# Feature sums of the two later norms in strips of 32 columns, in a two-layer hybrid decoder step on one Trainium2 core

## What is computed

```python
def layer_norm(x, g=None, b=None):
    xf = x.astype(jnp.float32)
    mu = jnp.mean(xf, axis=-1, keepdims=True)
    var = jnp.mean(jnp.square(xf - mu), axis=-1, keepdims=True)
    y = (xf - mu) * lax.rsqrt(var + LN_EPS)
    ...

def trunk_layer(x, c, pos, lw, st, mla_past):
    mod = jax.nn.silu(c) @ lw['w_ada'] + lw['b_ada']
    sh1, sc1, g1, sh2, sc2, g2 = jnp.split(mod[:, None, :], 6, axis=-1)
    u = x * (1.0 + sc1) + sh1
    mix, new_st = mixer_branches(u, pos, lw, st, mla_past)
    x = layer_norm(DEEPNORM_ALPHA * x + g1 * mix, lw['ln1_g'], lw['ln1_b'])
    u2 = x * (1.0 + sc2) + sh2
    f = (jax.nn.silu(u2 @ lw['w1']) * (u2 @ lw['w3'])) @ lw['w2']
    x = layer_norm(DEEPNORM_ALPHA * x + g2 * f, lw['ln2_g'], lw['ln2_b'])
    return x, new_st
```

## Time and profile before

| what | value |
|---|---|
| median of 3 runs | 1809.6 us (1809.22 to 1810.36) |
| the profiled execution | 1809.78 us, its span 1808.0 us |
| PE busy | 1703.8 us, 94% of the span |
| DVE, ACT, POOL busy | 809.4, 733.8, 705.7 us |
| granted clock of PE, mean | 0.971 of full speed |
| output projection, layer 0 | ends at about 635.8 us; norm 1 until about 655 us |
| second FFN product, layer 0 | ends at about 908.5 us |
| second FFN product, layer 1 | ends at about 1786.3 us; the span ends at 1808.0 us |

### The profile page before, as it was taken

The page is one execution under the profiler, slowest core; times in us unless marked ns, Lnnn a source line. Parts: engine busy times, 40 slices in busy tenths (PEclk is TensorE's granted clock), DMA queues, the critical chain, the costliest instruction groups (busy, mean ns, idle before and its releaser), DMA issues. The chain is left out here.

```text
span 1808.0 us, 29755 instructions
## 1 busy us (share of the span) xinstructions
PE 1703.8 (94%) x10994; PEld 1475.5 (82%) x10994; DVE 809.4 (45%) x1881; ACT 733.8 (41%) x1109; POOL 705.7 (39%) x446
## 2 busy tenths in 40 slices
PE   5999999999999979999979999999999999899997
PEld 2887889886667869998867879898866687799996
DVE  2364276656431353332255534866744323533223
ACT  2455534233434244442344554442344332444422
POOL 2344556636123423333323435655541234333331
PEclk8999999999999989999999999999999999899999
DMA  8365435337575344445624553362566834344440
GB/s 352 108 250 187 122 98 192 132 120 268 185 273 178 130 172 155 148 159 198 210 103 184 199 186 92 122 205 78 169 243 230 292 133 174 134 150 144 160 140 30
DMA packets 73522, 307.68 MB, mean 170 GB/s; under 512 B 15842, under 2 KB 25506, under 8 KB 43426
## 3 DMA queue, kind: packets, MB, share of 16 engines
q1 hardware_dynamic: 73378, 305.77, 48.3%
HBM read 291.81 MB, written 13.94 MB: 169 GB/s over the span
## 5 line engine op out<-in xcount | busy, mean ns | idle before, releaser
L2154 POOL TENSOR_TENSOR wlx<-ring,wh 128x1024 fp32r<-128x1024 f32 x172 | 409.6, 2381 | 659.2 <-ACT wh L1168 651.8
L454 PE MATMUL zps<-uhi,wh 128*128 128x320 f32 x1232 | 386.9, 326 | 0.2
L455 PE MATMUL zps<-ulo,wh 128*128 128x320 f32 x1232 | 372.4, 314 | 0.0
L1168 ACT ACTIVATE wh<-ring 128x1024 fp32r<-128x1024 f32 x172 | 182.2, 1060 | 363.5 <-PE zps L455 222.5
L2268 POOL TENSOR_TENSOR wlo<-ring,whi 128x1024 fp32r<-128x1024 f32 x66 | 160.1, 2426 | 318.2 <-ACT whi L1131 317.9
L454 PEld LDWEIGHTS zps<-uhi,wh 128*128 128x128 f32 x1232 | 238.5, 194 | 14.1 <-issue 7.7
L455 PEld LDWEIGHTS zps<-ulo,wh 128*128 128x128 f32 x1232 | 238.6, 194 | 1.2 <-issue 0.4
L938 PE MATMUL zps<-xhi,whi 128*128 128x320 f32 x688 | 214.0, 311 | 0.0
L939 PE MATMUL zps<-xlo,whi 128*128 128x320 f32 x688 | 213.8, 311 | 0.0
L940 PE MATMUL zps<-xhi,wlo 128*128 128x320 f32 x688 | 213.7, 311 | 0.0
L459 PE MATMUL zps<-uhi,wlx 128*128 128x320 f32 x1232 | 207.6, 311 | 0.0
(11 more groups left out here) (285 smaller groups left out, 2503.5 us busy)
## 6 DMA issues: line engine op xcount, KB each, us to landing
ring<-wpack_dram SPq DMA_DIRECT2D x222, 1024.0 KB, 4.9
arena<-cache_dram SPq DMA_DIRECT2D x128, 320.0 KB, 4.9
arena<-stateA_dram SPq DMA_DIRECT2D x2, 2064.0 KB, 9.5
o_cn_s<-arena SPq DMA_DIRECT2D x2, 2064.0 KB, 11.6
arena<-stateD_dram SPq DMA_DIRECT2D x2, 2048.0 KB, 11.7
o_ret_s<-arena SPq DMA_DIRECT2D x2, 2048.0 KB, 10.9
x<-x_dram SPq DMA_DIRECT2D x2, 1280.0 KB, 9.9
o_y<-x SPq DMA_DIRECT2D x4, 640.0 KB, 3.0
```

The lines of the kernel that those rows point to most:

```text
L454: nc.tensor.matmul(o, hi[:, k * P:(k + 1) * P], xh[:, k, :], start=k == 0, stop=False)
L455: last = nc.tensor.matmul(o, hi[:, k * P:(k + 1) * P], xl[:, k, :], start=False, stop=False)
L1168: nc.scalar.activation(wh[:, i, :], ring[:, g % RING, i * 1024:(i + 1) * 1024], ACT.Copy).then_inc(*ev("act_hq", (q, i), layer=layer))
L2154: G().tensor_tensor(low_ring(SPLIT[q])[:, half], ring_of(SPLIT[q])[:, half], wh[:, i, :], ALU.subtract).then_inc(*ev("pool_l", (q, i)))
```

## The change

The 128x128 matrix of ones is no longer the weight operand in the two norms. Instead:

- Each product uses 32 columns of ones, so its result has 32 rows, and goes into one of four strips of 32 partitions of the bank: tile k into strip k mod 4 (`strip_sum`). Each strip holds the sum of two tiles, the same in its 32 rows.
- ACT copies the bank of four strips to SBUF (`mean_strips` into std, and one more line in `squares` into tmp), and one more f32 product with a constant 128x128 matrix of 1/32 (`gather`) adds the four strips up and spreads the sum to all partitions. This holds for the mean and for the squares.
- In the second FFN product the products of the mean for k = 0 to 5 now stand behind the tiles d = 2 to 7, as they did in the output projection already; before, all came after the last tile. In both, k = 6 no longer waits for the last residual.
- `gather` takes the place of `ones` in the packed constants, but is loaded with the later part; the early part holds the identity alone. The ones are now taken from another constant that holds them anyway.

```diff
-    c["ones"] = np.ones((P, P), f)
+    c["gather"] = np.full((P, P), 1 / 32, f)
...
-        ident, ones = cs("ident"), cs("ones")
+        ident, gather = cs("ident"), cs("gather")
+        ones = cs("causal")[:, P:2 * P]
...
+                    def strip_sum(ps, src, k):
+
+                        g = 32 * (k % 4)
+                        return nc.tensor.matmul(ps[g:g + 32, 0:T], ones[:, 0:32], src[:, k, :], start=k < 4, stop=k >= 4)
+
                     def mean_part(which, k):
 
                         if k == 0:
-                            bank("m", ("mean", which), ("dve_r", ("mu", which, KC - 1)))
+                            bank("m", ("strips", which), ("act_n", ("strips", which)))
                         pe.wait_ge(*at("dve_r", ("r", which, k)))
-                        nc.tensor.matmul(banks[C.layer, ("mean", which)][:, 0:T], ones, u[:, k, :], start=k == 0, stop=False)
+                        return strip_sum(banks[C.layer, ("strips", which)], u, k)
 
                     def norm_sums(which):
-                        ps = banks[C.layer, ("mean", which)]
-                        pe.wait_ge(*at("dve_r", ("r", which, KC - 1)))
                         for k in range(KC - 2, KC):
-                            last = nc.tensor.matmul(ps[:, 0:T], ones, u[:, k, :], start=False, stop=k == KC - 1)
-                        last.then_inc(*ev("pe_m", ("mean", which)))
+                            last = mean_part(which, k)
+                        last.then_inc(*ev("pe_m", ("strips", which)))
+                        pe.wait_ge(*at("act_n", ("strips", which)))
+                        group("m", ("mean", which), ("dve_r", ("mu", which, KC - 1)), [(gather, std[:])])
                         if which == 1:
                             ada(20, 22, through=False)
                         elif C.layer + 1 < DEPTH:
                             ada(6, 7, through=False, layer=C.layer + 1)
-                        ps = bank("m", ("var", which), ("dve_r", ("xn", which, KC - 1)))
+                        ps = bank("m", ("squares", which), ("act_n", ("squares", which)))
                         for k in range(KC):
                             pe.wait_ge(*at("act_n", ("sq", which, k)))
-                            last = nc.tensor.matmul(ps[:, 0:T], ones, acc[:, k, :], start=k == 0, stop=k == KC - 1)
-                        last.then_inc(*ev("pe_m", ("var", which)))
+                            last = strip_sum(ps, acc, k)
+                        last.then_inc(*ev("pe_m", ("squares", which)))
+                        pe.wait_ge(*at("act_n", ("squares", which)))
+                        group("m", ("var", which), ("dve_r", ("xn", which, KC - 1)), [(gather, tmp[:, 1, :])])
...
-                    for k in range(KC - 2):
-                        mean_part(2, k)
+                        if d >= 2:
+                            mean_part(2, d - 2)
                     norm_sums(2)
...
-                        sp.dma_start(const[:, 0:2 * P], a["consts"][:, 0:2 * P]).then_inc(pre["pre_ident"], 16)
+                        sp.dma_start(const[:, 0:P], a["consts"][:, 0:P]).then_inc(pre["pre_ident"], 16)
...
-                            sp.dma_start(const[:, 2 * P:], a["consts"][:, 2 * P:]).then_inc(pre["pre_const"], 16)
+                            sp.dma_start(const[:, P:], a["consts"][:, P:]).then_inc(pre["pre_const"], 16)
...
+                    def mean_strips(which):
+                        go("act_n", ("strips", which), std[:], m(("strips", which))[:, 0:T], ACT.Copy)
+
                     def squares(which):
                         for k in range(KC):
                             act.wait_ge(*at("dve_r", ("mu", which, k)))
                             nc.scalar.activation(acc[:, k, :], u[:, k, :], ACT.Square).then_inc(*ev("act_n", ("sq", which, k)))
+                        go("act_n", ("squares", which), tmp[:, 1, :], m(("squares", which))[:, 0:T], ACT.Copy)
                         go("act_n", ("std", which), std[:], m(("var", which))[:, 0:T], ACT.Sqrt, bias=cs("eps")[:, 0:1], scale=1.0 / D_MODEL)
...
                     split(0)
+                    mean_strips(1)
                     ada(20, 22)
...
+                    mean_strips(2)
                     if C.layer + 1 < DEPTH:
                         ada(6, 7, C.layer + 1)
```

More of the change, by code:

```diff
@@ L1510, in _ @@
                         high(0, layer=C.layer + 1)
-                    go("act_n", "early", stats[:, 31:32], cs("ones")[:, 0:1], ACT.Sqrt)
+                    go("act_n", "early", stats[:, 31:32], ones[:, 0:1], ACT.Sqrt)
+                    mean_strips(2)
                     if C.layer + 1 < DEPTH:
```

## The result

| | median | runs |
|---|---|---|
| before | 1808.38 us | 10, 1801.21 to 1810.36 |
| with the change | 1815.06 us | 10, 1808.9 to 1822.48 |
| ratio | 1.0036 | 95% interval 1.0019 to 1.0053 |

A forecast was written before the change was run, and what follows sets the result against it. The prediction took TensorE (PE), busy 94% of the span, to bound the kernel. Norms 1 +4.0, norm 2 of layer 1 +3.6, of layer 0 +1.1, constants -0.15: +8.6 us on 1809.78, so 1818.4 us; range 1813 to 1822.

The forecast's parts named there:

- The price of a lone strip: PE time for one strip alone between full-width tiles: 0.86 us, being 0.55 plus 0.31 for changing width.
- Output projection, +1.55 each: Output projection before norm 1, both layers: five lone strips replace five full products, 5 x 0.31 = 1.55 us more each.
- The mean of norm 1 hidden behind adaLN block 21: Norm 1: the mean's chain grows 0.8 us, hidden because ACT's squares wait for block 21's late weights; cost 0.
- The uncovered table load, +0.47 each: Squares of norm 1, both layers: root's table load now follows ACT's strip copy, uncovered; root 0.47 us later each.
- p: Symbol for PE's cost of one lone strip between full-width tiles, taken as 0.86 us, bounds 0.55 and 0.90.
- The FFN of layer 1, 5p = +4.3, and the mean 0.96 earlier against the last residual: Layer 1, second FFN product: five strips add 4.3 us; norm 2's mean comes 2.13 us after the last residual, not 3.09.
- The FFN of layer 0: Layer 0, second FFN product: strips partly vanish in PE's three waits, +2.06 us; less 0.96 in norm 2, +1.1.
- Squares of the last norm, +0.28: Norm 2 of layer 1: root starts 2.22 us after the last square instead of 1.94, +0.28 us.
- rival 2: Clock falls in the norms' sparse PE chains: +2 to +4 us on top of the forecast, 1821.5 us; chance 0.2.
- Rival 1: A lone strip costs no more than a full product, 0.55 us: +3.0 us, 1812.8 us; chance 0.13.
- rival 3: Strips overlap with full-width neighbours, a lone one costing 0.13 us: -4.2 us, 1805.6 us; chance 0.04.
- The constants, -0.15: Kernel start: 64 KB fewer constants loaded ahead of the first adaLN blocks, saving 0.15 us, at most 0.3.

The follow-up runs named there:

- e4: Kernel before, with each product of norm 1's mean inside the output projection made as four 32-column strips side by side; ratio 0.9999 (0.9982 to 1.0016).
- e7: e1 with VectorE instead of ScalarE copying the strips of the squares; ratio to the kernel before 0.9953 (0.9934 to 0.9972), median 1799.42 us.
- e1: Changed kernel with all strips of the mean after the last tile, in output projection and second FFN product; ratio to the kernel before 0.9947 (0.9929 to 0.9965).
- e8: The kernel before, unchanged, profiled a second time; span 1811.9 us, 3.9 more than in the first profile.
- e9: The changed kernel, unchanged, profiled a second time; output projection tile again 4.37 us, no total time given.
- e2: e1 with the squares summed by eight full products, strips for the mean alone; ratio to the kernel before 0.9956 (0.9934 to 0.9978).
- e10: e2 again, unchanged, for a second profile; by the trace 7.4 us faster than the kernel before.

## Why the prediction was right

- *The price of a lone strip, 0.86 us*: measured at 0.86. It was worked out from two places of the kernel before, a 32x32 product and an adaLN block between full ones; neither is a lone strip of 128x32, so that their price carried over is a finding, too. e4 shows that it is the change of width and not the idle columns, which the prediction had only assumed. TensorEngine Tiling (Array Packing) of the Trainium skill says under Key Properties that a change of the tiling mode drains TensorE; the traces agree with it in that the change costs 0.31 us there and back. The factor of up to 4 in the same page of the Trainium skill (Theoretical Speedup) shows for strips side by side alone: in e4 four cost 0.87 us where one costs 0.86.
- *Output projection, +1.55 each*: +1.53 and +1.54.
- *The mean of norm 1 hidden behind adaLN block 21*: so it is, but with less to spare than the prediction thought. From the end of the last residual to the first square it is 5.14 us, against 5.21 before, though the mean comes 0.7 us later. The prediction took 1.33 us for today's chain, where its own row has 1.44, and so 0.8 us more for the new one, and it never set that against PE's wait for block 21. That wait was 0.80 and 0.71 us, and the 0.71 us more just fit in: there was luck in the 0.
- *The uncovered table load, +0.47 each*: +0.42 from the first square to the root. The way from the last square to the copy took 0.82 and not 0.88 us, the copy 0.44 and not 0.46; e7 shows that it is the load.
- *The FFN of layer 1, 5p = +4.3, and the mean 0.96 earlier against the last residual*: +4.27, and 0.94.
- *The FFN of layer 0*: +1.98 for +2.06, with strips in the first and third gap and the second gap gone. In the norm behind it -0.94 for -0.96 is two small misses that cancel: the mean came 0.88 us earlier against the last residual and not 0.96, and the squares took 0.07 us less where no change was forecast.
- *Squares of the last norm, +0.28*: +0.50 in both profiles of the change. e1, at the upper clock, has +0.21; the other 0.29 is the lower clock on the strips, while the product with the constant ran at the upper one. That is rival 2, in one of the four norms, and at less than a third of the price that the prediction gave it (e7: half of it).
- The 1.93 us of the earlier trace rows, from which rival 2 took its price, were read as the lower level. The profile shows a granted clock of 1.00 there, so no row shows that they are.
- *Rival 1 and rival 3* had p at 0.55 and 0.13; the rows give 0.86.
- *The constants, -0.15*: no run shows this term. The first adaLN block starts at 6.76 us before and 6.77 with the change, the second at 10.06 and 9.87, but at 10.24 in both second profiles (e8, e9).
- The total: +8.7 in the touched stretches of the profiles for +8.6, +6.5 us (3.4 to 9.6) in the measured times. The difference of 2 us is within the interval; the profiled execution of the change was one of its slower ones. What makes one execution 5 us longer than another is open in the main. Part of it is how long the lower clock lasts: the way from norm 1's root to residual 2 of the FFN, the same instructions before and after, took 203.93 us with 10.2 us of it at 0.50 and 205.16 with 17.1 in layer 0, and 202.97 with 10.2 and 201.43 with 6.8 in layer 1.

## What to carry to other kernels

Narrow products pay when they stand side by side, and a single one between products of full width costs more than the full product that it replaces: gather them into a gap that PE has anyway, here the wait for the last residual, and the same strips turn from 6.5 us of loss into 8 to 10 us of gain. A good part of that gain may come from the emptied stream of tiles and not from the strips; full products in the same gap should be tried first, which no run here did. The price of going over can be read before anything is built, from the starts of the neighbours of any narrow product that the program already has, and not from its duration. When a sum is moved forward, look also at what lay under its old place (a table load, a wait) and at how long its PSUM bank is now held.

## What the runs showed of the hardware that was not expected

- Going from products of 128 columns to strips of 32 and back costs 0.31 us with one strip and 0.32 us with four side by side. The strip or strips with it take 0.86 and 0.87 us of PE, where one full f32 product over 320 tokens takes 0.55 (the change, and e4).
- In a norm whose PE work is short pieces with pauses, the granted clock fell to 0.50 in some executions and not in others of the same kernel (e2 and e10). Eight full f32 products took 6.24 us and not 4.54 then, and the root came 1.7 us later; with strips for the same sum it came 0.3 us (the change) and 0.5 us (e7) later.
